# Gated attention: score tiles summed on VectorE in place of two denominator products, and the mean square one step later

## What is computed

```
w[s,t]   = exp(-max(spread[t] + a[s], 0)) for s <= t, else 0    # the decay
sc[s,t]  = (k_s . q_t) * w[s,t]
num[:,t] = sum_s v_s * sc[s,t]
den[t]   = sum_s sc[s,t]
h        = num / max(|den|, floor[t])
y        = h * rsqrt(mean(h*h) + eps) * mg * sigmoid(o)
```

```python
sc = jnp.einsum('bhtd,bhsd->bhts', qc, kc) * jnp.exp(dmat - m_t[..., None])
den = sc.sum(axis=-1) + w_inter * jnp.einsum('bhtd,bhd->bht', qc, n)
h = num / jnp.maximum(jnp.abs(den), jnp.exp(-m_t))[..., None]
...
hb = hb * lax.rsqrt(jnp.mean(hb * hb, axis=-1, keepdims=True) + NORM_EPS)
```

## Time and profile before

| | |
|---|---|
| time, median of 3 runs | 1713.92 us (1713.7 to 1713.99) |
| the profiled execution, its own time | 1713.66 us |
| its span in the trace | 1711.9 us |
| PE busy | 1698.0 us (99%) |
| weight loads (PEld), beside the products | 1363.1 us (80%) |
| DVE busy | 857.3 us (50%) |
| ACT busy | 649.7 us (38%) |
| POOL busy | 657.7 us (38%) |
| chain that ended last, PE's share | 92% |

### The profile page before, as it was taken

One profiled execution on the slowest core, in us unless ns is written; L12 is line 12 of the kernel. 1 busy time (PEld: TensorE's weight loads), 2 busy tenths in 40 slices (PEclk: granted clock), 3 DMA queues, 4 the chain that ended last, 5 costly groups with the idle time before them and its releaser, 6 DMA issues.

```text
span 1711.9 us, 23695 instructions
## 1 busy us (share of the span) xinstructions
PE 1698.0 (99%) x8121; PEld 1363.1 (80%) x8129; DVE 857.3 (50%) x1399; ACT 649.7 (38%) x1077; POOL 657.7 (38%) x276
## 2 busy tenths in 40 slices
PE   9999999999999999999999999999999999999998
PEld 7888777788888888888788766778888988888887
DVE  6723665574655552208497775542333775555013
ACT  6333444534222222327424576452223522222121
POOL 2444322244544444444343100234444344444443
PEclk9999999999999999999999999999999999999999
DMA  5354311223322223233422111113322222222321
GB/s 194 106 185 130 96 59 50 75 74 123 111 99 94 92 96 102 91 102 126 148 87 87 44 44 50 50 62 99 93 100 90 87 99 97 98 98 94 103 97 63
DMA packets 47635, 162.29 MB, mean 95 GB/s; under 512 B 5724, under 2 KB 7900, under 8 KB 47304
## 3 DMA queue, kind: packets, MB, share of 16 engines
q1 hardware_dynamic: 43872, 151.10, 26.5%
q10 hardware_dynamic: 3688, 10.20, 1.9%
HBM read 156.91 MB, written 4.76 MB: 94 GB/s over the span
## 4 chain that ended last, share of the span: by engine, by line
PE 92%; DVE 3%; ACT 2%; issue 1%; DMA 1%; ACTq 0%; SPq 0%; DVEq 0%
PE ps L482 27%; PE ps L484 26%; PE ps L483 26%; PE ps L681 2%; PE ps L663 2%; PE ps L1088 1%; PE ps L1087 1%; PE ps L1089 1%; PE ps L707 1%; PE ps L988 1%; PE ps L969 1%; PE ps L916 1%; DVE tmp L1864 1%; PE ps L947 0%; PE ps L689 0%
## 5 line engine op out<-in xcount | busy, mean ns | idle before, releaser
L426 POOL TENSOR_TENSOR w_lo<-w_raw,w_hi 128x1024 fp32r<-128x1024 f32 x261 | 644.5, 2471 | 1034.8 <-ACT w_hi L1158 1007.9
L482 PE MATMUL ps<-u_hi,w_hi 128*128 128x512 f32 x1352 | 545.2, 403 | 0.2 <-ACTq L1725 0.2
L484 PE MATMUL ps<-u_hi,w_lo 128*128 128x512 f32 x1352 | 527.4, 390 | 0.0
L483 PE MATMUL ps<-u_lo,w_hi 128*128 128x512 f32 x1352 | 526.7, 390 | 0.0
L1158 ACT ACTIVATE w_hi<-w_raw 128x1024 fp32r<-128x1024 f32 x271 | 285.4, 1055 | 395.6 <-PE ps L484 331.3
L482 PEld LDWEIGHTS ps<-u_hi,w_hi 128*128 128x128 f32 x1352 | 254.1, 188 | 57.9 <-issue 7.1
L484 PEld LDWEIGHTS ps<-u_hi,w_lo 128*128 128x128 f32 x1352 | 253.8, 188 | 53.8
L483 PEld LDWEIGHTS ps<-u_lo,w_hi 128*128 128x128 f32 x1352 | 254.3, 188 | 51.9 <-issue 2.4
L1558 ACT ACTIVATE tmp<-tmp 128x512 f32<-128x512 f32 x44 | 27.8, 632 | 213.2 <-DVEq L2214 213.2
L2224 DVE TENSOR_TENSOR a_lo<-tmp,a_hi 128x512 f32 (+1 forms) x44 | 106.1, 2412 | 4.7
L482 PE MATMUL ps<-a_hi,w_hi 128*128 (+1 forms) x264 | 102.9, 390 | 0.0
(11 more groups left out here) (382 smaller groups left out, 2382.7 us busy)
## 6 DMA issues: line engine op xcount, KB each, us to landing
w_raw<-stream SPq DMA_DIRECT2D x277, 512.0 KB, 3.5
g_rep<-g_one ACTq DMA_DIRECT2D x1, 2560.0 KB, 13.2
spread<-m_rows ACTq DMA_DIRECT2D x4, 512.0 KB, 4.5
tmp<-tmp ACTq DMA_DIRECT2D x32, 64.0 KB, 3.7
bias<-g_rep ACTq DMA_DIRECT2D x1, 2048.0 KB, 10.6
outT<-hT SPq DMA_DIRECT2D x16, 128.0 KB, 1.8
hT<-xT SPq DMA_DIRECT2D x3, 512.0 KB, 7.7
mem_in<-memT ACTq DMA_DIRECT2D x1, 1024.0 KB, 4.8
```

The lines of the kernel that those rows point to most:

```text
L426: pool.tensor_tensor(w_lo[:, slot], w_raw[:, slot], w_hi[:, slot].bitcast(F32), ALU.subtract)\
L482: pe.matmul(out, wh, xh, start=start, stop=False)
L483: pe.matmul(out, wh, xl, start=False, stop=False)
L484: return pe.matmul(out, wl, xh, start=False, stop=stop)
```

## The change

The denominator is no longer summed by PE alone. The first 128 queries only see the score tile of step 0, so `ones` times its first 128 columns is their denominator. For the queries from 128 on, DVE adds the four score tiles up in `em_sum` (a new tile of 128 x 512), and one product of 384 columns follows in step 3. `ml_sc` of step 3 is signalled after the last add.

Around it the order changes. On PE `mean_square(h-1)` moves from step 0 to step 1. On ACT `decay(h, 2)` comes ahead of `head_rms(h-1)`, and `head_out(h-1)` behind the decays of the next head. On DVE the copy of unit `2h-1` moves from step 0 to behind step 1, `head_y(h-1)` from behind step 1 to behind step 3, and `head_low` by one head: `head_low(h-2)` in step 0 of head `h`, and `head_low(2)` in turn 0 of the next attention.

```diff
+        em_sum = ar("em_sum", [P, T], F32, 68)
...
                         x = em[2 + j % 2][:, 0:T - j * P]
-                        pe.matmul(ps[:, 4, j * P:T], vb[:, j, h * P:h * P + P], x, start=j == 0, stop=j == QT - 1)
-                        pe.matmul(ps[:, 5, j * P:T], ones, x, start=j == 0, stop=j == QT - 1)\
-                          .then_inc(named("ml_nd"), 1)
+                        m = pe.matmul(ps[:, 4, j * P:T], vb[:, j, h * P:h * P + P], x, start=j == 0, stop=j == QT - 1)
+                        if j == 0:
+                            m = pe.matmul(ps[:, 5, 0:P], ones, x[:, 0:P], start=True, stop=True)
+                        if j == QT - 1:
+                            m = pe.matmul(ps[:, 5, P:T], ones, em_sum[:, P:T], start=True, stop=True)
+                        m.then_inc(named("ml_nd"), 1)
                     if i < QT:
                         quarter("gate1a", 8 * h + 1 + i)
-                    if i == 0 and h >= 1:
+                    if i == 1 and h >= 1:
                         mean_square(h - 1)
...
                 feed_after(FIRST["gate1a"] + 2 * h)
+                decay(h, 2)
                 if h >= 1:
                     head_rms(h - 1)
-                decay(h, 2)
-                if h >= 1:
-                    head_out(h - 1)
                 decay(h, 3)
...
                 if h + 1 < NHB:
                     decay(h + 1, 0)
                     decay(h + 1, 1)
+                if h >= 1:
+                    head_out(h - 1)
                 act.wait_ge(named("ml_h"), h + 1)
...
                 for i in range(QT):
-                    if i == 0 and h >= 1:
-                        filled("gate1a", 2 * h - 1, lambda k: g1a[k][:, :])
...
                     step(dve.tensor_tensor(em[2 + i % 2][:, 0:n], ps[:, 2 + i % 2, 0:n], w[:, 0:n], ALU.mult))
                     dve.sem_inc(bank_free[2 + i % 2], 1)
-                    dve.sem_inc(named("ml_sc"), 1)
-
+                    if i < QT - 1:
+                        dve.sem_inc(named("ml_sc"), 1)
+                    if i == 0 and h >= 2:
+                        head_low(h - 2)
+                    if i >= 1:
+                        x, later = em_sum[:, i * P:T], em[2 + i % 2][:, 0:n]
+                        step(dve.tensor_tensor(x, em[2][:, P:T] if i == 1 else x, later, ALU.add))
+                    if i == QT - 1:
+                        dve.sem_inc(named("ml_sc"), 1)
                     if i == 1 and h >= 1:
+                        filled("gate1a", 2 * h - 1, lambda k: g1a[k][:, :])
+                    if i == QT - 1 and h >= 1:
                         head_y(h - 1)
-                    if i == 2 and h >= 1:
-                        head_low(h - 1)
...
                 if g == 0:
                     filled("gate1a", 7, lambda k: g1a[k][:, :])
+                    head_low(NHB - 2)
```

## The result

The changed kernel takes 1720.95 us (median of 6 runs, 1719.37 to 1722.24) against 1714.05 for the kernel before (6 runs, 1713.7 to 1715.11): a ratio of 1.0039, 95% interval 1.0029 to 1.0049. It is **6.9 us slower**. The sign was forecast; the time, 1718.6, was 2.35 too low, and the measured median lies 0.45 above the range. The profiled execution took 1720.62 with a span of 1718.8 (before: 1713.66 and 1711.9).

What follows compares the result with a forecast made beforehand. TensorE was taken as the bound, busy 1698.0 of 1711.9 us. Removed products -5.16, head 0 +2.8, heads 2 and 3 +3.8 and the next attention +3.3 gave +4.7 us: 1718.6, range 1717.0 to 1720.0.

Steps and rivals of the forecast that it cites:

- The sign: Whole kernel: slower was forecast, chance 0.62, against same 0.21 and faster 0.17.
- Removed products, 1.29 a head: TensorE, four heads: ones products of 512 and 256 columns go, saving 1.29 us a head, 5.16 in all.
- Head 0, +1.5: Head 0, steps 2 and 3: -1.29 saved, two added TensorE waits of 1.4 us each, +1.5 net.
- head_y and the subtraction, VectorE's chain 2.0 late, 1.9 of pause: Step 3: moved head_y meets GpSimd's subtraction; VectorE's chain starts 2.0 us late, PE waits 1.9 in heads 2 and 3.
- The same moment: Step 3: head_y's first instruction and GpSimd's subtraction start together at about +1.0 us; either order frees VectorE at about +4.8.
- The next attention, 3.3: First turns after head 3: TensorE waits of 1.4, 0.6, 0.9 and 0.4 us, together 3.3.
- case C: Rival, TensorE's clock: pauses up to 2 us drop it to 1.2 GHz; ten us of work would give 1728; chance 0.04.
- Case A: Rival, the heads: port decides nothing, adds and head_y take 0.3 to 0.75 each; -3.9 us, 1710.1; chance 0.17.
- case B: Rival, the heads: head_y escapes GpSimd's subtraction, the rest as forecast; -1.1 us, 1712.8; chance 0.14 with its like.
- The sum without a fall: Whole kernel, no term for a clock drop: +4.7 us against the kernel before.

Runs made afterwards that it cites:

- the last experiment: Changed kernel with head_y's root in PSUM, second weight unit rounded later, head_low(2) before the last gate copy, rope(7) split: 1707.57 us, ratio 0.9963.
- the filled kernel: Changed kernel with useless TensorE products placed where PE would wait in heads 0, 2 and 3: 1718.94 us, +5.1 against the kernel before.
- the order alone: Changed kernel without its adds and with all four ones products back, only the queue reordering left: 1720.42 us, +6.5 against the kernel before.
- the first experiment: Changed kernel with head_y's root and the product between its two instructions in PSUM: 1712.57 us, -1.3 against the kernel before.
- the adds alone: Kernel before with the changed kernel's adds and two remaining ones products, nothing moved: 1721.83 us, +8.0 against the kernel before.
- the second profile of the changed kernel: Changed kernel run again with nothing altered: median 1722.42 us, ratio 1.0047 to the kernel before; its profiled execution took 1722.63 us.

## Why the prediction was right or wrong

- **Removed products, 1.29 a head:** right. Head 1, the only one without a pause, is 1.45 shorter, and the last experiment gives all 5.2 back.
- **Head 0, +1.5:** right, +1.6, with both pauses where they were put (1.68 and 1.12 idle, of which 0.21 was there before; 1.4 and 1.4 more were forecast).
- **head_y and the subtraction, VectorE's chain 2.0 late, 1.9 of pause:** right, 2.02 in both heads. "The same moment" was 0.03 us, and POOL went first; it made no difference, as said. Reading from PSUM or moving the subtraction takes the pause away, so the cause is shown and not only argued.
- **The next attention, 3.3:** 3.65 from the table (1.5 + 0.8 + 1.35). Right in each wait, a little small.
- **The step that failed is case C**, the clock. The text set it aside with a chance of 0.04 because "in the rows the granted clock never falls". But the rows of before hold no pause of 2 us in the heads: they could not speak on it. And the row it was read from can't show a fall of 3.4 us: it reads 9 throughout in the changed kernel as well. Its mechanism was there, but its price was not worked out for one fall, and the sum held no term for it: it is 1.7 us each, with one in the first profiled execution of the changed kernel and two in the second. Head 3 shows it (+2.4 instead of +0.6), and the filled kernel shows that the pauses bring it. The forecast's sum plus one fall is 6.4, with two 8.1; the two profiled executions, at 7.0 and 8.8 above the kernel before, are these.
- The Trainium skill's rule ("TensorE: Matmul & The Clock Gate", section "A second HAM failure mode: psum-queue depth-cycling", frequent short idles between groups of matmuls can make the clock swing) was named as speaking for case C. These runs agree in part. The mean clock is 0.91 in stretches of 20 us that hold one pause of 1.8 to 2.0 us, and 1.00 with the pauses filled; but it is 1.00 too in head 2 of the first profile, with a pause of 2.02, and in the order alone, with 1.6.
- Case A (no contention) is refuted by the 2.97 and 1.97 us rows; case B did not occur, but the first experiment is its arithmetic made real: -1.1 forecast there, -1.3 measured. The sum without a fall was a little small: +5.1 with the pauses filled.
- The range was too narrow at the top by the omitted term: with a fall or two as part of the likeliest case it would have had to reach 1722.

What stays open: why two pauses of 1.5 and 1.6 us in the heads (the order alone) left the clock up, while one of 1.8 in each of heads 1 to 3 (the adds alone) brought it down three times; why the pause of 1.7 us in head 0 brought no fall in any trace; and why the same pause of 2.0 in head 2 brought one in the second profile of the changed kernel and none in the first. Where in the sequence a pause must lie was not tried.

## What to carry to other kernels

Lay each VectorE instruction with two SBUF inputs against GpSimd's intervals before moving it, not only against VectorE's own queue: the meeting costs the whole rest of the other's run, and putting one operand in PSUM (where the bank allows it) removes it (0.76 us for the instruction in place of 2.97). Where a pause appears on a TensorE that was always busy, add a term for the clock: here 1.7 us for each fall, on top of the pause. And removed work is gained only once the chains beside it still arrive: the same denominator gave +6.9 us and -6.3 us, by the order around it and the place of one operand.

## What the runs showed of the hardware

A subtraction of 2.4 us on GpSimd and a VectorE instruction with two SBUF inputs do not overlap in either order: issued second, VectorE's took 2.97, 1.97 and 2.06 for 512, 256 and 128 columns, against 0.75, 0.42 and 0.29 alone. When both started within 0.03 us, GpSimd's ran at its usual 2.40. With one operand in PSUM VectorE's ran beside GpSimd's at 0.76 and 0.69. Where a subtraction was issued while a VectorE instruction with two SBUF inputs ran, it was the subtraction that took longer (2.85), and the next VectorE instruction waited for it in turn (2.75). Falls of the clock to 1.2 GHz lasted about 3.4 us each, in the kernels with TensorE pauses of 1.8 to 2 us in the heads, and began 0 to 0.9 us after the end of a pause; their number differs between executions of one kernel (one and two in the two profiles of the changed kernel). That is a part of its spread of 2.3 to 2.9 us and not all of it: the kernel before, without such pauses, spreads over 1.4 to 2.1, and the version with all out of the way over 0.12.
